# A three-block kernel on one Trainium2 core: the decay's sum as the exponential's bias, a scan scaled group by group, weight loads handed out later, and short products that fill TensorE's waits

## The chip, the cores and the metric

The kernel runs on one core of one Trainium2 chip. The metric is the device time of one execution in microseconds (us), the median over several runs. All tensors are float32.

## The reference, cut to what matters

The program computes two blocks. The first is attention plus a gated delta rule and a feed-forward layer over 256 tokens of width 1024. The second has two layers, each a mixer followed by a mixture of 16 experts; layer 0 works on 512 tokens (256 of context, 256 latent), layer 1 keeps the latent ones. Between the parts stand RMS norms. The change is for the most part in layer 0's mixer, a state-space scan in chunks of 128 tokens, run in both directions:

```python
la = (dt * a_neg).reshape(bsz, nc, SSD_CHUNK, ng, rep)
acum = jnp.cumsum(la, axis=2)
xdt = xs * dt[..., None]
to_end = jnp.exp(acum[:, :, -1:] - acum)
chunk_states = einsum("bcsgn,bcsgr,bcsgrp->bcgrpn", bc, to_end, xdt)
s_final, s_in = lax.scan(_carry_step, s0, (chunk_decay, chunk_states))
seg = acum[:, :, :, None] - acum[:, :, None, :]
decay = jnp.exp(jnp.where(causal, seg, -jnp.inf))
cb = jnp.einsum("bclgn,bcsgn->bclsg", cc, bc)
y_diag = jnp.einsum("bclsg,bclsgr,bcsgrp->bclgrp", cb, decay, xdt)
y_off = jnp.einsum("bclgn,bcgrpn,bclgr->bclgrp", cc, s_in, jnp.exp(acum))
return (y_diag + y_off), s_final
```

Beside it the kernel computes the modulation `silu(cond) @ mod_w + mod_b` of layer 1, whose weight is 24 MB.

## The kernel before, in words

**Stages.** The program is a chain of stages (`stage`, L227). A stage holds one instruction list per engine, with semaphores between them. Its end is a barrier for all engines (the branch at L231): the next stage starts when the slowest of TensorE, VectorE, ScalarE, GpSimd and SyncE has run its list, and SyncE's list is the issue of weight loads.

**Loads.** `Feed` has six slots of 1 MB. Every weight is cut into units of 1 MB, in the order in which TensorE takes them. `run` issues the units of one plan, each when the unit six before it has been used, and at its end `run_ahead` issues up to six units of the next plan (`most`). `run_part` (L310) does a piece of a plan that runs beside other stages. The modulation's plan is 24 units, two for each of 12 chunks of 512 columns (`modulate`, L2202). A chunk counts `mods_done` up by two when its products are done.

**The scan's four parts** (function `ssd`), in time order:
- Preparation: transposes, the step sizes `dt` (a softplus with chunks 0 and 1 of the modulation beside it), then a stage that makes the cumulated decay `acum` on TensorE with triangular matrices, copies it, and takes three exponentials. In that stage TensorE also does chunk 2, and SyncE issues modulation units 6 to 11.
- Main scan: 16 steps q = (t, g), four token tiles by four head groups. `prepare(q)` on TensorE makes C·B (L2320) and, for two directions and four heads, the decay's sum spread over rows (L2327). VectorE's `args(q)` subtracts the column's own sum and adds the causal mask, eight instructions of 128x128 (L2358). ScalarE takes two exponentials of 128x512 (L2387). VectorE multiplies by C·B (L2373), and TensorE makes 16 products of 64 columns (L2344) with `x_dt`, which VectorE makes for all 1024 columns of a tile when its first group comes up (L2368): it waits there until the last group's products have read the old one.
- State stage: eight steps n, each a chunk state, its decay and its part of the output; beside it modulation chunks 3 to 11 (`chunks_at`), three transposes of them (`turned_at`), and SyncE issues units 12 to 23 and six units of the output projection `ab_w_out`.
- `even_output`: gate, norm and output projection.

**Where TensorE waits.** `rmsnorm` (L467) has TensorE sum squares (L518), waits for root and reciprocal, and spreads the root (L523); with a residual VectorE then works for all eight tiles, without one and with `tail` the next stage does that part. `gated_head_norm` (L750) is the same per head. `route` chooses experts in a long VectorE chain and then counts in a stage of its own. At the end of `experts` the rows go to DRAM and come back gathered before TensorE turns them (L3115).

TensorE's granted clock has two levels here, 2.4 GHz (1.00 in the rows) and 1.2 GHz (0.50).

## Time and profile before

| what | value |
|---|---|
| median of 3 runs | 2445.96 us (2444.46 to 2446.03) |
| the profiled execution's own time | 2446.49 us |
| its span | 2444.7 us |
| TensorE busy, matmul | 2194.3 us (90%) |
| VectorE, ScalarE, GpSimd busy | 947.7, 483.3, 97.5 us |
| mean granted clock of TensorE | 0.946 of full speed |

How to read it: TensorE is busy nine tenths of the span, so an instruction saved on another engine is worth something only in a stage in which TensorE waits for that engine. A busy TensorE is not one at full speed: a clock of 0.50 in a stretch doubles each product. What a stage costs beyond that is read at its boundary, where the last engine's list ends.

### The profile page before, as it was taken

What the parts mean: (1) busy time and instruction counts of PE and PEld (TensorE: products, weight loads), DVE (VectorE), ACT (ScalarE), POOL (GpSimd) and SP (SyncE); (2) the same over time, 40 slices, a digit from 0 to 9 for tenths busy, and PEclk for the clock granted to TensorE, in tenths of its full rate; (3) what the DMA queues carried; (4) which work ended last, traced back from release to release, by engine and by line L of the source; (5) the groups of instructions that cost most, each with busy time, mean ns of one, the idle gap of its engine ahead of it and who ended that gap; (6) DMA issues with size and microseconds to landing.
All of it is one profiled execution on the core that took longest, in us unless ns stands there. A gap on an engine that the chain in (4) does not pass through costs nothing. (4 is left out here: it accounts for less than half of the span.)

```text
span 2444.7 us, 35746 instructions
## 1 busy us (share of the span) xinstructions
PE 2194.3 (90%) x14716; PEld 1546.8 (63%) x14716; DVE 947.7 (39%) x1997; ACT 483.3 (20%) x926; POOL 97.5 (4%) x122
## 2 busy tenths in 40 slices
PE   7999988798999889999787997999959999879884
PEld 6887887786888754444586444555537567745452
DVE  2267234312110239999485313211140555232112
ACT  0032522100000020003330102000031766121001
POOL 0000022100111000000000001000010000000000
PEclk8999999998999899999998998999969999989987
DMA  8443374243789622221308525999952222359993
GB/s 251 142 151 109 116 226 138 69 154 122 279 305 324 215 87 86 69 86 65 126 1 266 200 77 217 362 380 391 350 168 69 74 83 85 154 212 416 418 418 146
DMA packets 241237, 464.82 MB, mean 190 GB/s; under 512 B 14146, under 2 KB 195316, under 8 KB 216372
## 3 DMA queue, kind: packets, MB, share of 16 engines
q1 hardware_dynamic: 213120, 401.58, 46.6%
q0 software_dynamic: 12672, 46.14, 4.8%
q10 hardware_dynamic: 15284, 14.83, 1.9%
q8 instruction: 115, 1.88, 0.3%
q14 instruction: 46, 0.38, 0.0%
HBM read 412.84 MB, written 49.68 MB: 189 GB/s over the span
## 5 line engine op out<-in xcount | busy, mean ns | idle before, releaser
L2061 PE MATMUL bank<-hn,weights 128*128 128x512 f32 x640 | 277.5, 596 | 2.3 <-ACT hn L457 2.3
L2061 PEld LDWEIGHTS bank<-hn,weights 128*128 128x128 f32 x640 | 122.4, 191 | 156.0 <-issue 155.2
L2116 DVE SCALAR_TENSOR_TENSOR conv_sum<-mixer_then_weights_ahead,vec,conv_sum 128x572 f32<-128x572 f32 x240 | 175.0, 832 | 0.0
L625 PE MATMUL bank<-u,weights 128*128 128x256 f32 x768 | 170.8, 379 | 0.9 <-PEq L231 0.9
L3574 PE MATMUL bank<-hn,weights 128*128 128x512 f32 (+1 forms) x512 | 169.2, 488 | 0.0
L625 PEld LDWEIGHTS bank<-u,weights 128*128 128x128 f32 x768 | 144.8, 190 | 24.1 <-issue 5.4
L1655 PE MATMUL bank<-u,weights 128*128 128x256 f32 x704 | 155.6, 383 | 1.0 <-DVE u L438 1.0
L1655 PEld LDWEIGHTS bank<-u,weights 128*128 128x128 f32 x704 | 135.2, 192 | 19.9 <-issue 1.1
L3574 PEld LDWEIGHTS bank<-hn,weights 128*128 128x128 f32 x512 | 96.0, 190 | 65.3 <-issue 58.4
L2561 PE MATMUL bank<-mixer_then_weights_ahead,weights 128*128 128x512 f32 x256 | 110.6, 592 | 0.0
L3039 PE MATMUL bank<-weights,hn 128*32 128x128 f32 (+1 forms) x1344 | 99.8, 333 | 9.2 <-DMA weights<-in_moe_w_gate 6.7
L3240 DVE COPY hn<-bank 128x256 f32<-128x256 f32 (+1 forms) x41 | 15.4, 376 | 235.4 <-PE bank L3048 120.3
L3039 PE MATMUL bank<-mixer_then_weights_ahead,hn 128*64 128x256 f32 (+1 forms) x1120 | 99.0, 346 | 4.6 <-DMA mixer_then_weights_ahead<-in_moe_w_gate 4.6
L3039 PEld LDWEIGHTS bank<-weights,hn 128*32 128x32 f32 (+1 forms) x1344 | 62.6, 124 | 43.8 <-issue 22.3
L681 PE MATMUL bank<-u,weights 128*128 128x256 f32 x384 | 86.0, 388 | 4.7 <-DVE u L438 4.7
L3039 PE MATMUL bank<-weights_ahead,hn 128*32 128x128 f32 (+1 forms) x1120 | 74.2, 319 | 16.7 <-DMA weights_ahead<-in_moe_w_gate 13.9
L3039 PEld LDWEIGHTS bank<-mixer_then_weights_ahead,hn 128*64 128x64 f32 (+1 forms) x1120 | 62.3, 127 | 38.6 <-issue 12.0
L2561 PEld LDWEIGHTS bank<-mixer_then_weights_ahead,weights 128*128 128x128 f32 x256 | 48.3, 190 | 59.7 <-issue 59.7
L681 PEld LDWEIGHTS bank<-u,weights 128*128 128x128 f32 x384 | 74.9, 195 | 15.6 <-DVEq L689 4.9
L726 PE MATMUL bank<-ffn_hidden,weights 128*128 128x256 f32 x352 | 76.2, 379 | 1.9 <-PEq L231 1.9
L3039 PEld LDWEIGHTS bank<-weights_ahead,hn 128*32 128x32 f32 (+1 forms) x1120 | 47.5, 120 | 42.8 <-issue 24.1
L726 PEld LDWEIGHTS bank<-ffn_hidden,weights 128*128 128x128 f32 x352 | 66.8, 190 | 11.3 <-issue 2.3
(555 smaller groups left out, 3074.9 us busy)
## 6 DMA issues: line engine op xcount, KB each, us to landing
weights<-in_mod_w SPq DMA_DIRECT2D x48, 1024.0 KB, 8.0
weights<-in_w_in SPq DMA_DIRECT2D x36, 1024.0 KB, 5.3
token_rows<-o_b POOLq DMA_DIRECT2D x68, 512.0 KB, 7.6
weights<-in_moe_w_gate SPq DMA_DIRECT2D x24, 1024.0 KB, 25.1
weights<-in_moe_w_up SPq DMA_DIRECT2D x24, 1024.0 KB, 18.4
weights<-in_moe_w_down SPq DMA_DIRECT2D x24, 1024.0 KB, 20.0
weights<-in_ab_w_in SPq DMA_DIRECT2D x20, 1024.0 KB, 5.3
mixer_then_weights_ahead<-in_moe_w_gate SPq DMA_DIRECT2D x20, 1024.0 KB, 17.9
```

What stands on the lines that cost most here:

```text
L625: last = pe.matmul(bank(n), unit[:, k, m * P:(m + 1) * P], x(k), start=k == 0, stop=k == ktiles - 1)
L681: last = pe.matmul(kit.bank[n % 4][:, 0:T], unit[:, k, m * P:(m + 1) * P], x(k), start=k == 0, stop=k == DC - 1)
L726: last = pe.matmul(kit.bank[m][:, 0:T], unit[:, k, m * P:(m + 1) * P], x(at + k), start=at + k == 0, stop=at + k == total - 1)
L1655: last = pe.matmul(kit.bank[which + n % 2][:, 0:T], unit[:, k, m * P:(m + 1) * P], x(k), start=k == 0, stop=k == DC - 1)
L2061: last = pe.matmul(tile_bank(n)[:, :], unit[:, k, lane * P:(lane + 1) * P], hn[:, k, :], start=k == 0, stop=k == DC - 1)
L2116: ins = dve.scalar_tensor_tensor(s, x, w, s, ALU.mult, ALU.add)
L2561: last = pe.matmul(kit.bank[n % 4][:, 0:T2], unit[:, k, (n % 2) * P:(n % 2 + 1) * P], x(k), start=k == 0, stop=k == DC - 1)
L3039: last = pe.matmul(out, x[:, k, half, :], columns, start=half == 0 and k == 0, stop=half == 1 and k == 3)
L3240: dve.tensor_copy(ht[:, 0:4 * r], h_bank[:, 0:4 * r]).then_inc(h_copied, 1)
L3574: last = pe.matmul(bank, units[key][:, k, lane * P:(lane + 1) * P], hn[:, k, cols], start=k == 0, stop=k == DC - 1)
```

## The change

It has four parts.

1. **Decay.** The sum is kept negated (`minus_a_sum`). In the main scan VectorE only adds the mask, one 128x512 instruction per direction; the own sum enters as the bias of the exponential, so ScalarE has four of 128x128 per direction.
2. **x_dt by group.** Two instructions of 128x256 per step, made two steps ahead, in place of two of 128x1024 per tile.
3. **Loads and chunks.** Modulation units 6 to 13 are issued in the main scan's stage, 14 to 23 in the state stage, which issues only two units of `ab_w_out`; `feed.rest` issues the other four at the start of `even_output`. Chunk 3 is computed in the main scan at step 4.
4. **Fills.** `keep_busy` issues products of the identity with 256 columns, whose results nobody reads, at waits of TensorE.

```diff
+    def rest(self, sp):
+        _, per, source = self.plans[self.at]
+        for j in range(self.left, min(SLOTS, per)):
+            self.load(sp, source(0, j))
+        self.left = SLOTS
-    def run_part(self, sp, matmuls_done, first, last):
+    def run_part(self, sp, matmuls_done, first, last, most_ahead=SLOTS):
...
+def keep_busy(kit, pe, products, bank):
+    for _ in range(products):
+        pe.matmul(kit.bank[bank][:, 0:WIDE], kit.c("ident"), kit.const[:, 0:WIDE], start=True, stop=True)
@@ NormTail.wait (each norm with tail)
+        if c == 0:
+            keep_busy(self.kit, pe, 1, 5)
@@ rmsnorm, tensor
+                keep_busy(kit, pe, 1, 5)
                 for c in order:
...
                 last.then_inc(summed, 1)
+                keep_busy(kit, pe, 2, 5)
                 pe.wait_ge(inverted, 1)
...
                 last.then_inc(spread, 1)
+                if not tail:
+                    keep_busy(kit, pe, 6, 5)
@@ gated_head_norm, tensor: before the sums, and before the wait for the reciprocals
+                keep_busy(kit, pe, 2, 7)
...
+                keep_busy(kit, pe, 2, 7)
@@ ssd, the decay's sum
-                        v.link(dve, dve.tensor_copy(acum[:, :, :], ps))
+                        v.link(dve, dve.tensor_scalar(minus_a_sum[:, :, :], ps, -1.0, None, ALU.mult))
...
-                    @block.sync
-                    def _(sp):
-                        feed.run_part(sp, kit.mods_done, SLOTS, 2 * SLOTS)
@@ main scan
+                    @block.sync
+                    def _(sp):
+                        feed.run_part(sp, kit.mods_done, SLOTS, 2 * SLOTS + 2)
...
-                            pe.wait_ge(xdt_ready, t + 1)
+                            if q == 4:
+                                pe.wait_ge(y_copied, q)
+                                modulate(kit, pe, cond, 3, early_chunk(3))
+                            pe.wait_ge(xdt_ready, q + 1)
...
-                                for j in range(4):
-                                    at = d * 16 + 4 * g + j
-                                    ins = dve.scalar_tensor_tensor(m[:, q % 2, d, j, :], kit.bank[2 + 2 * (q % 2) + d][:, j * P:(j + 1) * P],
-                                                                   acum[:, t, at:at + 1], kit.c(("neg_f", "neg_r")[d]), ALU.subtract, ALU.add)
-                                ins.then_inc(args_ready, 1)
+                                dve.tensor_tensor(m[:, q % 2, d], kit.bank[2 + 2 * (q % 2) + d][:, :].rearrange("p (j n) -> p j n", j=4),
+                                                  kit.c(("neg_f", "neg_r")[d]).unsqueeze(1).broadcast_to([P, 4, P]), ALU.add).then_inc(args_ready, 1)
+                        def x_dt(q):
+                            t, g = steps[q]
+                            at = slice(g * 256, (g + 1) * 256)
+                            if q >= 4:
+                                dve.wait_ge(y_ready, q - 3)
+                            for d in range(2):
+                                ins = dve.tensor_tensor(by_head(xdt[:, d, at]), by_head(xt[:, t, at]),
+                                                        spread(dt[:, t, 16 * d + 4 * g:16 * d + 4 * g + 4], 4), ALU.mult)
+                            ins.then_inc(xdt_ready, 1)
...
-                                act.activation(m[:, q % 2, d], m[:, q % 2, d], ACT.Exp).then_inc(exp_ready, 1)
+                                for j in range(4):
+                                    at = d * 16 + 4 * g + j
+                                    ins = act.activation(m[:, q % 2, d, j, :], m[:, q % 2, d, j, :], ACT.Exp, bias=minus_a_sum[:, t, at:at + 1])
+                                ins.then_inc(exp_ready, 1)
@@ state stage
-                chunks_at = {0: (3,), 2: (4, 5), 3: (6, 7), 5: (8, 9, 10), 6: (11,)}
-                turned_at = {1: 0, 4: 1, 7: 2}
+                chunks_at = {1: (4, 5), 2: (6,), 3: (7,), 5: (8, 9), 6: (10, 11)}
+                turned_at = {0: 0, 4: 1, 7: 2}
...
-                        feed.run_part(sp, kit.mods_done, 2 * SLOTS, 2 * LATER_CHUNKS)
+                        feed.run_part(sp, kit.mods_done, 2 * SLOTS + 2, 2 * LATER_CHUNKS, 2)
@@ even_output, sync
+                feed.rest(sp)
                 sp.wait_ge(gated, DC)
@@ route: after the transposes; after the counts
+                keep_busy(kit, pe, 3, 6)
...
+                keep_busy(kit, pe, 2, 6)
@@ experts: at the start; at the end
+                keep_busy(kit, pe, 1, 0)
                 gather(0, 0, CAP)
...
                 pe.wait_ge(x_copied, count + (S + 1))
+                keep_busy(kit, pe, 24, 0)
                 pe.wait_ge(y_copied, count + S)
```

**What moves.** SyncE's list from the preparation's last stage to the output stage, before (a stage starts at the branch with a line of its own and ends at the branch L231; `L261` is a load into a slot of `Feed`):

```order
L2292 UNCONDITIONAL_BRANCH
L261 DMA weights<-in_mod_w 128x8x256 x6
L231 UNCONDITIONAL_BRANCH
L2411 UNCONDITIONAL_BRANCH
L261 DMA weights<-in_mod_w 128x8x256 x12
L261 DMA weights<-in_ab_w_out 128x8x256 x6
L231 UNCONDITIONAL_BRANCH
L2539 UNCONDITIONAL_BRANCH
L2857 DMA ven_mixer_then_weights_ahead<-in_moe_w_gate 128x2048 x2
L2857 DMA ven_mixer_then_weights_ahead<-in_moe_w_up 128x2048 x2
L2857 DMA ven_mixer_then_weights_ahead<-in_moe_w_down 128x2048 x2
```

and with the change:

```order
L2332 UNCONDITIONAL_BRANCH
L261 DMA weights<-in_mod_w 128x8x256 x8
L231 UNCONDITIONAL_BRANCH
L2445 UNCONDITIONAL_BRANCH
L261 DMA weights<-in_mod_w 128x8x256 x10
L261 DMA weights<-in_ab_w_out 128x8x256 x2
L231 UNCONDITIONAL_BRANCH
L2569 UNCONDITIONAL_BRANCH
L261 DMA weights<-in_ab_w_out 128x8x256 x4
L2890 DMA ven_mixer_then_weights_ahead<-in_moe_w_gate 128x2048 x2
L2890 DMA ven_mixer_then_weights_ahead<-in_moe_w_up 128x2048 x2
L2890 DMA ven_mixer_then_weights_ahead<-in_moe_w_down 128x2048 x2
```

The stage that held six modulation loads alone has no SyncE list any more; two loads moved from the state stage to the main scan, and four of `ab_w_out` to the stage after the next barrier.

VectorE in the main scan, before (`decay_cb<-bank,...` is the argument, `x_dt` the scaled x, `decay_cb<-decay_cb,c_b` the product with C·B):

```order
L2358 SCALAR_TENSOR_TENSOR decay_cb<-bank,a_sum,const 128x128 x8
L2368 TENSOR_TENSOR x_dt<-ven_mixer_then_weights_ahead,dt 128x1024 x2
L2373 TENSOR_TENSOR decay_cb<-decay_cb,c_b 128x512 x2
L2358 SCALAR_TENSOR_TENSOR decay_cb<-bank,a_sum,const 128x128 x8
L2373 TENSOR_TENSOR decay_cb<-decay_cb,c_b 128x512 x2
L2358 SCALAR_TENSOR_TENSOR decay_cb<-bank,a_sum,const 128x128 x8
L2373 TENSOR_TENSOR decay_cb<-decay_cb,c_b 128x512 x2
```

and with the change:

```order
L2381 TENSOR_TENSOR decay_cb<-bank,const 128x512 x2
L2390 TENSOR_TENSOR x_dt<-ven_mixer_then_weights_ahead,dt 128x256 x4
L2401 TENSOR_TENSOR decay_cb<-decay_cb,c_b 128x512 x2
L2381 TENSOR_TENSOR decay_cb<-bank,const 128x512 x2
L2390 TENSOR_TENSOR x_dt<-ven_mixer_then_weights_ahead,dt 128x256 x2
L2401 TENSOR_TENSOR decay_cb<-decay_cb,c_b 128x512 x2
L2381 TENSOR_TENSOR decay_cb<-bank,const 128x512 x2
```

Eight small instructions per step became two, and `x_dt` comes in pieces between the argument and the product.

TensorE at the end of the second `experts` and in the last norm, before (L3115 turns the gathered rows, L518 sums squares, L523 spreads the root, L393 turns the result):

```order
L3115 MATMUL bank<-const,weights_ahead 128x128 x16
L231 UNCONDITIONAL_BRANCH
L510 UNCONDITIONAL_BRANCH
L518 MATMUL bank<-squares,const 32x64 x32
L523 MATMUL bank<-rstd,const 128x64 x4
L231 UNCONDITIONAL_BRANCH
L385 UNCONDITIONAL_BRANCH
L393 MATMUL bank<-const,hn 128x128 x16
L231 UNCONDITIONAL_BRANCH
```

and with the change (L429 is a fill; L3150, L536, L542 and L400 are the four above):

```order
L429 MATMUL bank<-const 128x256 x24
L3143 REGISTER_ALU
L3150 MATMUL bank<-const,weights_ahead 128x128 x16
L231 UNCONDITIONAL_BRANCH
L527 UNCONDITIONAL_BRANCH
L429 MATMUL bank<-const 128x256
L536 MATMUL bank<-squares,const 32x64 x32
L429 MATMUL bank<-const 128x256 x2
L542 MATMUL bank<-rstd,const 128x64 x4
L429 MATMUL bank<-const 128x256 x6
L231 UNCONDITIONAL_BRANCH
L392 UNCONDITIONAL_BRANCH
```

A run of 24 fills stands before the turned rows, and one, two and six in the norm.

## Rows read from the trace of the kernel before

**Rows 1.** The page: its first line and TensorE's line of part 1.
```profile
span 2444.7 us, 35746 instructions
PE 2194.3 (90%) x14716; PEld 1546.8 (63%) x14716; DVE 947.7 (39%) x1997; ACT 483.3 (20%) x926; POOL 97.5 (4%) x122
```

**Rows 2.** By stretch: length, PE, PEld, DVE, ACT, POOL busy (count), clock, DMA share, GB/s.
```profile
1198.80:1207.50 8.70, 0.00 (x0) 0.00 (x0) 0.01 (x1) 0.00 (x0) 0.00 (x0) 0.71 1.09 348
1207.50:1282.70 75.20, 66.34 (x544) 65.32 (x544) 62.95 (x168) 27.93 (x64) 0.00 (x0) 0.93 0.10 30
1282.70:1340.30 57.60, 45.80 (x684) 38.07 (x684) 34.74 (x52) 1.98 (x5) 0.00 (x0) 0.87 0.80 256
```

**Rows 3.** Timeline at the first boundary: start us, duration us, engine, line; idle before.
```profile
1197.99 0.29 ACT L2300 ACTIVATE to_end<-to_end 128x128 f32<-128x128 f32 x1
1198.19 0.29 ACT L2301 ACTIVATE a_total_exp<-a_total_exp 128x128 f32<-128x128 f32 x1
...
1198.51 0.29 DVE L2280 TENSOR_TENSOR to_end<-to_end,dt 128x128 f32<-128x128 f32 x1 [0.78 <-ACT a_total_exp L2301]
...
1196.58 10.55 SPq L261 DMA_DIRECT2D weights<-in_mod_w  x3
```

**Rows 4.** Groups by line: count, busy us, mean ns of one, idle before.
```profile
L2358 DVE SCALAR_TENSOR_TENSOR decay_cb<-bank,a_sum,const 128x128 f32<-128x128 f32 x128 | 34.6, 344 | 11.9 <-PE bank L2327 11.9
...
L2387 ACT ACTIVATE decay_cb<-decay_cb 128x512 f32<-128x512 f32 x32 | 20.2, 632 | 40.3 <-DVE decay_cb L2358 40.3
...
L2373 DVE TENSOR_TENSOR decay_cb<-decay_cb,c_b 128x512 f32<-128x512 f32 x32 | 21.7, 687 | 1.2
...
L2368 DVE TENSOR_TENSOR x_dt<-mixer_then_weights_ahead,dt 128x1024 f32<-128x1024 f32 x8 | 9.4, 1221 | 3.2 <-PE bank L2344 3.2
...
L587 PE MATMUL bank<-hgrn_out,weights 128*128 128x256 f32 x128 | 27.9, 380 | 1.0 <-PEq L231 1.0
...
L1234 ACT ACTIVATE scores<-scores,softmax_small 128x128 f32<-128x128 f32 x8 | 3.2, 403 | 0.1
```

**Rows 5.** Timeline of the main scan on TensorE: products of groups, and its end.
```profile
1224.21 1.90 PE L2344 MATMUL bank<-x_dt,decay_cb 128*128 128x64 f32 x16
...
1228.01 1.90 PE L2344 MATMUL bank<-x_dt,decay_cb 128*128 128x64 f32 x16
...
1233.61 1.97 PE L2344 MATMUL bank<-x_dt,decay_cb 128*128 128x64 f32 x16 [1.64 <-issue]
...
1278.11 3.64 PE L2344 MATMUL bank<-x_dt,decay_cb 128*128 128x64 f32 x16 [1.49 <-issue]
```

**Rows 6.** Timeline of the state stage's last loads and the second boundary.
```profile
1327.20 18.11 SPq L261 DMA_DIRECT2D weights<-in_ab_w_out  x6
...
1324.32 2.74 PE L2208 MATMUL bank<-weights,cond 128*32 128x128 f32 x64 [3.09 <-DMA weights<-in_mod_w]
...
1345.76 3.62 PE L2552 MATMUL bank<-const,hn 128*128 128x128 f32 x16 [5.79 <-PEq L231]
```

**Rows 7.** By stretch, columns as in rows 2: stages that get fills.
```profile
470.40:484.70 14.30, 7.70 (x64) 6.46 (x65) 9.44 (x16) 4.67 (x10) 0.00 (x0) 0.76 0.01 1
571.10:594.90 23.80, 12.67 (x156) 10.28 (x157) 14.31 (x38) 4.04 (x11) 2.27 (x3) 0.57 0.27 94
...
1488.90:1502.80 13.90, 11.06 (x40) 7.29 (x42) 5.08 (x25) 0.00 (x0) 3.93 (x4) 0.51 0.23 93
...
1776.20:1792.10 15.90, 0.01 (x1) 0.03 (x1) 1.98 (x2) 1.24 (x1) 6.27 (x7) 0.60 0.90 282
...
2103.90:2116.40 12.50, 8.74 (x60) 7.50 (x53) 9.11 (x15) 1.79 (x6) 0.00 (x0) 0.60 0.00 1
...
2144.30:2175.20 30.90, 19.21 (x144) 11.15 (x146) 17.52 (x70) 9.15 (x19) 0.00 (x0) 0.67 0.42 174
2404.00:2416.40 12.40, 0.00 (x0) 0.00 (x0) 1.98 (x2) 1.24 (x1) 3.76 (x4) 0.63 0.56 181
2416.40:2444.70 28.30, 11.86 (x104) 9.85 (x104) 11.66 (x26) 5.08 (x9) 0.00 (x0) 0.56 0.11 42
```

More of the change, by code:

```diff
@@ L316, in run_part @@
         if last == per:
-            self.run_ahead(sp, per, lambda back: sp.wait_ge(matmuls_done, back + 1))
+            self.run_ahead(sp, per, lambda back: sp.wait_ge(matmuls_done, back + 1), most_ahead)
     def run_ahead(self, sp, units, used_up, most=SLOTS):
@@ L415, in _, with __init__ @@
                 act.copy(dst, src).then_inc(copied_a, 1)
+def keep_busy(kit, pe, products, bank):
+    for _ in range(products):
+        pe.matmul(kit.bank[bank][:, 0:WIDE], kit.c("ident"), kit.const[:, 0:WIDE], start=True, stop=True)
 class NormTail:
     SIGNALS = ("norm_scaled", "norm_by_a", "norm_by_v")
-    def __init__(self, x, root, parts, whole, by_vector):
+    def __init__(self, kit, x, root, parts, whole, by_vector):
+        self.kit = kit
         self.x, self.root, self.parts, self.whole = x, root, parts, whole
@@ L562, in rmsnorm @@
             if tail:
-                return NormTail(x, root, parts, whole, by_vector_last)
+                return NormTail(kit, x, root, parts, whole, by_vector_last)
 def project_programs(kit, x, ktiles, T, widths, evacuate):
@@ L1983 @@
 LATER_CHUNKS = 12
-MOD_EARLY = 3
 def even_units(ab):
@@ L2229, in ssd @@
             xt, bt = out.rearrange("p c t -> p (c t)").rearrange("p (t d) -> p t d", t=NT), new("b_tokens", NT, 512)
-            dt, la, acum, eac, etot, toend = [new(n, NT, 32) for n in ("dt", "log_decay", "a_sum", "a_exp", "a_total_exp", "to_end")]
+            dt, la, minus_a_sum, eac, etot, toend = [new(n, NT, 32) for n in ("dt", "log_decay", "minus_a_sum", "a_exp", "a_total_exp", "to_end")]
             turn(kit, [([xbc[:, c + j, t * P:(t + 1) * P] for j in range(4)], xt[:, t, c * P:(c + 4) * P])
@@ L2264, in ssd @@
                 softplus(kit, flat(dt[:, :, :]), flat(dt[:, :, :]), NT * 32,
-                         lambda pe: [modulate(kit, pe, cond, b, early_chunk(b)) for b in range(MOD_EARLY - 1)])
+                         lambda pe: [modulate(kit, pe, cond, b, early_chunk(b)) for b in range(2)])
                 with stage(nc, "la_ready", "sums_ready", "copied", "finished", "v") as (block, la_ready, sums_ready, copied, finished, vsem):
@@ L2289, in _ @@
                         last.then_inc(sums_ready, 1)
[L2290 to L2294 removed]
+                        modulate(kit, pe, cond, 2, early_chunk(2))
                     @block.scalar
@@ L2355, in args @@
                                     dve.wait_ge(y_ready, q - 1)
[L2356 to L2360 removed]
+                                dve.tensor_tensor(m[:, q % 2, d], kit.bank[2 + 2 * (q % 2) + d][:, :].rearrange("p (j n) -> p j n", j=4),
[9 more added lines that the diff above has]
+                            ins.then_inc(xdt_ready, 1)
                         args(0)
+                        for q in range(2):
+                            x_dt(q)
                         for q, (t, g) in enumerate(steps):
[L2364 to L2369 removed]
                             dve.wait_ge(cb_copied, q + 1)
@@ L2376, in _ @@
                                 args(q + 1)
+                            if q + 2 < len(steps):
+                                x_dt(q + 2)
                     @block.scalar
```

20 lines of the change are left out of this document (5 added, 15 removed).

## The prediction

> **What bounds the kernel now.** I read the page first: TensorE is busy 2194 of 2445 us [rows 1], so 250 us are left, and only an edit that shortens a wait of TensorE, removes its own work, or lifts its clock can show. Then I cut the span into stretches and looked for those where TensorE stands still or is granted half a clock. Three of them lie side by side in the scan. At the preparation's end TensorE does nothing for 8.70 us while DMA runs at 348 GB/s; the main scan takes 75.20 us at 30 GB/s, with TensorE busy 66.34 and VectorE 62.95; the state stage goes back to 256 GB/s with TensorE busy 45.80 of 57.60 [rows 2]. So loads bind the first and the third, and the one between has the DMA engines almost free. Last I read the timeline at the seams. At 1198.5 to 1198.8 the last real work of the preparation ends, but the issue of loads lasts from 1196.58 for 10.55 us, to 1207.1, and the barrier waits for it [rows 3]. At the second seam the six output loads are being issued for 18.11 us, to 1345.3, 3.0 us each, while TensorE's last product before is at 1327 and its next at 1345.76 [rows 6].
>
> **Part 1, the loads at the first seam.** The stage loses its SyncE list, so it ends with VectorE's last instruction at 1198.8 and not at 1207.1. Some 0.7 us of hand-over stay, as now (1207.1 to 1207.5, then the first product). That is **-8.0 us**. The eight loads that go into the main scan take 8 x 3.0 = 24 us of its 75, where nothing else is loaded; SyncE's list there ends after chunk 3, long before the stage does. What is late next at this seam is nothing: TensorE, ScalarE and VectorE end within 0.5 us of one another.
>
> **Part 2, the main scan.** Now TensorE sets the step: two groups of products stand 3.80 us apart (1224.21, 1228.01). Once per tile it waits for `x_dt`: the next group comes at 1233.61, 5.60 us later [rows 5], since both 1221-ns instructions [rows 4] start only when the old `x_dt` is read. Three tiles have this, 3 x 1.8 = **-5.4 us** once `x_dt` is made in pieces two steps ahead. The start of this stage runs at half clock after the idle 8.7 us (clock 0.71 there, 0.93 over the stage); without the idle most of this goes, **-2.5 us**. At the stage's end the last products take 3.64 us and not 1.90, at half clock [rows 5]; that should stay in part, and I take **-1 us**. Against this stands chunk 3, about 64 products, which takes 2.74 us at the clock of its row [rows 6] and some 2 at full clock, with half a microsecond of waiting: **+2.5 us**.
>
> Then the new pace. VectorE's step was eight of 344 ns (start to start about 0.27), two of 687 and a quarter of two 1221 [rows 4]: about 4.2 us in the mean. After it is two arguments at 0.69, two products at 0.69, and two pieces of 128x256 that I put at 0.42, between the two sizes: 3.6 us, under 3.80. ScalarE's chain is what may be late next. It had two of 632 ns. Now it has eight of 128x128 with a bias. One such takes 403 ns [rows 4]; two 128x128 of that engine without a bias start 0.20 us apart though each is 0.29 long, so 0.09 overlaps [rows 3], which gives 8 x 0.31 = 2.5 us, or with no overlap 3.2. The ends of the step's loop (argument of one direction 0.69, hops of about 0.3, product 0.64 to 0.69) run partly beside it. With overlap the loop is about 4.0 us against 3.80, which costs up to 3 us over 16 steps and may be hidden by the double buffer of `m`; without it, 4.9 us, or +13 in all. I take **+1**, nearest the row that shows overlap on the same engine, and keep -1 and +13 as ends. Part 2 is then -5.4 - 2.5 - 1 + 2.5 + 1 = **-5.5 us**.
>
> The Trainium skill ("VectorE: DVE Perf Modes", section "The TRN2 errata — SBUF-src ops pay a fixed extra latency per instruction") says that on trn2 each instruction of VectorE and ScalarE that reads SBUF pays a fixed cost, so that small tiles are dear; that speaks for the two wide arguments and against four exponentials in place of one. The 403 ns for a quarter of a 632-ns tile agree. The same notes ("ScalarE: Activation LUTs", section "Step-by-step: what each stage is for") put the overlap of two such instructions at about 93 ns, with which eight would take an estimated 2.45 us and the loop stays near TensorE's pace.
>
> **Part 3, the state stage and the second seam.** Now they last from 1282.7 to 1345.7, 63 us, and 18 loads of 3.0 us (54 us) with the wait for the first free slots fill them. After, ten modulation loads are due; they start when chunk 4 has freed slots, some 13 us in, and last 30 us. With the last load's landing (1.5), chunk 11 (2), its copy and the third transposing that makes about 48.5 us. The other chain there, VectorE's, had 34.74 us busy [rows 2] and waits for TensorE in each of eight steps, 45 us by estimate, just below. So **-14 us**, range -10 to -16. The four loads left go to the start of `even_output`, 12 us; the first two units are there, and one lasts TensorE 16 blocks by 512 tokens, 16 x 2 x 0.436 = 14 us (0.436 us for a product of 256 columns: 27.9 us / 64 pairs of records [rows 4]). I cost the loads at nothing; if that cover were gone, 3 to 6 us. After a shorter seam `even_output` starts warm: the 16 turns that took 3.62 us [rows 6] would take half, **-1.7 us**.
>
> Loads and scan together: -8.0 - 5.5 - 14 - 1.7 = **-29 us**, range -20 to -34.
>
> **Part 4, the fills.** A fill does no work; it can pay only by keeping TensorE's clock at 2.4 GHz for the products behind it. The most a stretch can give is its TensorE busy time less what it would be at full clock: busy x (1 - clock). From [rows 7] that is: a head norm 1.9, layer 0's residual norm 5.4, route 5.4, the next head norm 3.5, a long pair of norm and route 6.3 us, the last norm 5.2; 27.7 us, and some 7 more in two stretches of the first half that read like these. Not all comes. Head norms get two plus two fills for 6.6 us of standing still in several pieces: they should hold. In the residual norms the six fills last 6 x 0.436 = 2.6 us, less than half of VectorE's closing piece, which I estimate at 6 us of its 14.31 [rows 7], and the main scan lost its clock with idles of only 1.5 us [rows 5]; so some will still fall. The 24 fills last 10.5 us at full clock, against waits of 15.90 us in layer 0 and 12.40 us in layer 1 [rows 7]: in layer 0 5.4 us stay idle and the clock probably falls, in layer 1 2 us, and the norm behind it may start warm. I take half of the 34: **-17 us**. The low end: with the clock half anyway, a fill takes 0.87 us and stands ahead of work that is waited for. Six of them, 5.2 us, may outlast VectorE's closing piece where there is no residual, as at the last norm; 24 would take 20.9 us, 5 over the one wait and 8.5 over the other. At the norms that costs 0.4 to 2 us each.
>
> The sum is -29 - 17 = -46 us from the profiled execution's own 2446.5 us, which is 0.5 above the median: **2400 us**.
>
> **The rivals.** (A) The forecast, 62%: 2400, own range 2386 to 2413. (B) The fills give nothing: TensorE's clock falls in their gaps anyway and what they delay eats what they hold; 2446 - 29 = 2417 us. For it speaks the fall at the main scan's end with such short idles; against it that the main scan, with an idle of 1.64 us once per tile [rows 5], holds 0.93 over its length. 16%. (C) The fills hold nearly all, and the scan's part is at its best: 2446 - 34 - 28 = 2384 us, 12%. (D) The scan's part is small, because ScalarE's eight exponentials run without overlap (+12) or because the loads in the main scan reach back into steps; with the fills' 17 that gives 2446 - 17 - 17 = 2412, with weak fills 2422; 7%. (E) Slower: the 24 fills run at half clock in both layers. They begin after the last expert's products, while scatter and gather wait; if the clock falls before they end, the turned rows stand behind 20.9 us of fills, +5 and +8.5 us, and the norms lose 5 to 7 more; about +20. It decides only if parts 1 to 3 give less than that, for which the loads would have to be late by 10 us in the state stage. 2446 + 20 - 18 = 2448 at best, and to be over 0.2% above, 2452. 3%. That the change does not do what it says for the loads is excluded by the order of SyncE's list; for the fills it is rival B.
>
> **The numbers.** Likeliest 2400. The range takes A whole, B and most of D above and half of C below: 2378 to 2421. A measurement of this kernel can tell 0.2%, 4.9 us, from no change. Faster than that: A, B, C, D and a little of E, 0.95; within it 0.02; slower 0.03.
>
> **What would show it.** In the changed profile: the idle stretch of 8.7 us before the main scan is gone and the modulation loads lie beside it; groups of products stand 3.8 to 4.0 us apart with no 5.6 among them (4.9 throughout would be D); ScalarE's exponentials start 0.30 us apart; the state stage with its seam lasts 47 to 51 us; the output stage does not wait for its third unit. For the fills: granted clock of 0.9 and above in the head norms, 0.7 to 0.9 in the residual norms, and the gathered rows of the second layer turned at once after the wait. I am wrong in the main if the clock in the norms stays at 0.6, or if a stretch with fills is longer than before.

## The result, and the profile after

The changed kernel takes 2409.01 us, the median of four runs (2405.23 to 2412.61), against 2445.99 before (2444.46 to 2447.47). The ratio is 0.9848, 95% interval 0.9836 to 0.9860: 37 us faster, where 46 were forecast. The profiled execution took 2411.49 us, 2.5 above its median. Executions of one kernel differ by up to 13 us, so medians and intervals carry what follows, and one trace tells where time went, not to the microsecond how much.

The page of the changed kernel, beside [rows 1]:

```profile
span 2409.7 us, 36244 instructions
...
PE 2237.2 (93%) x14956; PEld 1578.7 (66%) x14956; DVE 936.1 (39%) x1925; ACT 502.1 (21%) x1021; POOL 97.7 (4%) x122
...
L429 PE MATMUL bank<-const 128*128 128x256 f32 x240 | 71.3, 438 | 29.7 <-PEq L231 20.8
```

TensorE is 43 us busier in a span that is 35 us shorter: 71.3 us of its work are fills. The three stretches of the scan, beside [rows 2], are the hand-over at the first seam, the main scan, and the state stage with the second seam (length, PE, PEld, DVE, ACT, POOL busy, clock, DMA share, GB/s):

```profile
1198.50:1200.50 2.00, 1.62 (x33) 1.12 (x25) 0.00 (x0) 0.00 (x0) 0.00 (x0) 0.50 0.00 0
1200.50:1269.00 68.50, 65.45 (x608) 64.73 (x608) 52.12 (x96) 47.29 (x160) 0.00 (x0) 0.95 0.39 124
1269.00:1322.20 53.20, 43.05 (x621) 35.67 (x621) 34.77 (x52) 1.86 (x5) 0.00 (x0) 0.90 0.75 238
```

The 8.70 us in which TensorE stood still are gone; the main scan went from 75.20 to 68.50 us with one chunk more in it; the state stage and seam went from 63 to 53. Inside the main scan, by timeline (products of groups) and by group of lines:

```profile
1210.80 1.90 PE L2369 MATMUL bank<-x_dt,decay_cb 128*128 128x64 f32 x16
...
1214.59 1.90 PE L2369 MATMUL bank<-x_dt,decay_cb 128*128 128x64 f32 x16
...
1264.55 3.65 PE L2369 MATMUL bank<-x_dt,decay_cb 128*128 128x64 f32 x16 [1.84 <-issue]
```

```profile
L2420 ACT ACTIVATE decay_cb<-decay_cb,minus_a_sum 128x128 f32<-128x128 f32 x128 | 39.2, 388 | 9.8 <-DVE decay_cb L2381 9.8
...
L2390 DVE TENSOR_TENSOR x_dt<-mixer_then_weights_ahead,dt 128x256 f32<-128x256 f32 x32 | 12.0, 419 | 0.0
```

The pace is 3.79 us, where [rows 5] have 3.80; none of the three gaps of 5.60 is left. One gap of 5.77 us stands in the scan, at step 4, and that is chunk 3:

```profile
1218.39 1.90 PE L2369 MATMUL bank<-x_dt,decay_cb 128*128 128x64 f32 x16
...
1224.16 2.00 PE L2369 MATMUL bank<-x_dt,decay_cb 128*128 128x64 f32 x16
```

One exponential is 388 ns long, and eight take 2.45 us, start to start 0.30, which is what the overlap in [rows 3] said. The clock still falls at the tail: 3.65 us for the last products, as before.

**Where the 35 us of the two traces lie.** I lined up the instructions of VectorE that both programs have. The difference of their start times (after less before) grows through a stretch by what that stretch gained. The same was done later for two experiments (the changed kernel without fills, the kernel before with fills alone):

| stretch (time before, us) | changed | no fills | fills alone |
|---|---|---|---|
| start to 1190 | -1.8 | -2.5 | -5.1 |
| first seam, with the start of the scan, to 1209 | -7.9 | -11.7 | -2.0 |
| main scan to 1283 | -3.9 | -5.0 | +1.6 |
| state stage and second seam to 1346 | -10.7 | -9.7 | +0.3 |
| `even_output` to 1460 | -0.7 | +1.2 | 0.0 |
| norm and route, layer 0, to 1505 | -1.5 | +1.1 | -1.5 |
| experts, layer 0, to 1640 | -1.5 | +1.2 | +2.3 |
| experts, layer 0, to 1765 | +3.5 | +0.2 | +1.0 |
| combining and norm, to 1830 | -0.3 | +1.7 | +1.1 |
| head norm, layer 1, to 2118 | -2.6 | -1.4 | -2.6 |
| norm and route, layer 1, to 2177 | -3.0 | +0.4 | -3.0 |
| experts and combining, layer 1, to 2422 | -1.2 | -0.2 | -1.9 |
| last norm | -2.2 | 0.0 | -2.1 |
| sum | -33.7 | -24.7 | -11.8 |

The table is one execution of each kernel. Entries of 1 to 3 us come and go: up to 1190 us the kernel without fills has the instructions of the kernel before, and its entry is -2.5 all the same. The execution of the fills alone that was traced, 2434.25 us, is 5 us faster than that kernel's median, so its sum of -11.8 is too good by as much. In the changed kernel's trace chunk 2 ran at half clock (0.50 in the first row above; it took 3.64 us, a chunk at full clock 1.95), which cost some 2 us at the first seam.

**The state stage** is one of the two terms that came short, the other being the fills (timeline of SyncE and TensorE):

```profile
1283.07 24.72 SPq L261 DMA_DIRECT2D weights<-in_mod_w  x10
```
```profile
1316.92 3.23 PE L2230 MATMUL bank<-weights,cond 128*32 128x128 f32 x64 [4.08 <-DMA weights<-in_mod_w]
...
1322.19 1.94 PE L2583 MATMUL bank<-const,hn 128*128 128x128 f32 x16 [0.68 <-PEq L231]
```

The first of ten loads is issued 14 us into the stage, when chunk 4 has freed its slots; chunk 11 waits 4.08 us for the last of them and then runs mostly at half clock (3.23 us in place of 1.95). The next stage starts 0.68 us after the barrier and warm, 1.94 us for the turns in place of 3.62 [rows 6].

**The stretches with fills**, beside [rows 7] in the same order (their six here: first head norm, residual norm, route of layer 0, combining of layer 0, norm and route of layer 1, last norm):

```profile
472.70:486.50 13.80, 9.33 (x72) 7.28 (x73) 9.35 (x17) 4.66 (x10) 0.00 (x0) 0.88 0.00 1
572.90:592.80 19.90, 15.33 (x183) 11.72 (x184) 14.30 (x38) 4.04 (x11) 2.27 (x3) 0.91 0.23 69
1463.60:1476.10 12.50, 12.13 (x46) 8.29 (x48) 5.10 (x25) 0.00 (x0) 2.98 (x3) 0.59 0.16 64
1751.50:1768.70 17.20, 13.23 (x50) 11.14 (x49) 1.98 (x2) 2.42 (x2) 7.27 (x7) 0.80 0.91 288
...
2116.80:2144.70 27.90, 21.71 (x164) 13.15 (x166) 17.52 (x70) 9.13 (x19) 0.00 (x0) 0.88 0.47 194
...
2386.00:2409.70 23.70, 11.99 (x122) 9.39 (x122) 11.66 (x26) 4.83 (x9) 0.00 (x0) 0.86 0.12 46
```

The clock rose in every one (0.57 to 0.91, 0.67 to 0.88, 0.56 to 0.86, but in layer 0's choice only 0.51 to 0.59). The first head norm gives 0.5 us, the combining of layer 0 is 1.3 us longer, counted to the first turned rows, and the others give 1.4 to 4.6.

The traces of all runs give this more firmly. Take eight of the stages that get fills: five norms or head norms, the choice of layer 0, the long pair in layer 1, and layer 1's combining with the last norm. From a stage's first instruction to the next stage's, the eight together take 164.2 to 168.3 us in the four kernels without fills (164.2 in the one that differs from the change by its fills alone) and 146.8 to 152.3 in the ten with fills (149.0 in the changed kernel). So inside their own stages the fills give about 15 us. The experiments show that less than that reaches the end.

### The profile page after: what moved, and what is told of

It reads as the page before. It is cut to its first block and busy times, and to the rows that moved or that the text cites. A ratio compares the mean times of both kernels' runs of the same rounds, so it can differ in the third digit from the quotient of the medians.

```text
span 2409.7 us, 36244 instructions
## 1 busy us (share of the span) xinstructions
PE 2237.2 (93%) x14956; PEld 1578.7 (66%) x14956; DVE 936.1 (39%) x1925; ACT 502.1 (21%) x1021; POOL 97.7 (4%) x122
## 5 line engine op out<-in xcount | busy, mean ns | idle before, releaser
L429 PE MATMUL bank<-const 128*128 128x256 f32 x240 | 71.3, 438 | 29.7 <-PEq L231 20.8
L429 PEld LDWEIGHTS bank<-const 128*128 128x128 f32 x240 | 47.9, 214 | 44.7 <-issue 33.7
```

The lines of the kernel that those rows point to most:

```text
L429: pe.matmul(kit.bank[bank][:, 0:WIDE], kit.c("ident"), kit.const[:, 0:WIDE], start=True, stop=True)
```

## The experiments

Each was timed beside the kernel before on the same chip, and its ratio is to that kernel. Its distance from the change is a difference of two medians. The intervals reach 3 to 6 us to either side, so a distance under some 5 us is not shown by the times, and has only the traces behind it. Theory at the start: loads and scan give about 25 us and do so through the two seams and the three stalls; fills give about 10, since a half clock costs only where TensorE sets the pace. Rivals: the fills are worth their forecast 17 or nothing, and the parts lean on one another.

**No fills.** `keep_busy` issues nothing.

```diff
-    for _ in range(products):
+    for _ in range(0):
```

> The changed kernel without any fill (240 matmul records of them gone). Theory, from the two traces: the fills give 9 to 11 us, all after the scan, since a half clock costs only where TensorE itself sets the pace; so 2418 to 2420 us, and the scan with both seams as in the changed kernel. Rival 1, the prediction's term: fills give 17 us, 2426. Rival 2: the fall of the clock is not stopped by them and the gain after the scan has another source: 2409 to 2412.

Measured: 2420.68 us (ratio 0.9897, 0.9880 to 0.9914). The fills give 11.7 us, loads and scan 25.2. The trace's mean clock is 0.949 against 0.970 with fills. As time at the half level that is 2 x 0.051 x 2419 = 247 us against 2 x 0.030 x 2410 = 145: **102 us of half clock were taken away for 12 us of time**.

**Fills alone** on the kernel before (all calls of `keep_busy`, nothing else).

> The kernel before with the fills alone. Theory: the same 9 to 11 us as when they are taken away from the changed kernel, 2435 to 2437 us. Rival 1: 17 us, 2429. Rival 2: nothing, or up to 3 us slower, 2446 to 2449, if what they give depends on the other parts.

Measured: 2439.27 us (0.9970, 0.9958 to 0.9981), a gain of 6.7. That is 2 to 4 us less than expected, and well under 17. The 6.7 and the 11.7 overlap in their intervals, so these runs do not show that the fills are worth more in the changed kernel.

**Loads alone**: part 3 of the change on the kernel before.

> The kernel before with the loads and chunks handed out as in the change (chunk 3 in the main scan, four output loads in even_output), but with the old decay, x_dt per tile and no fills. Theory: the first seam gives 8, the state stage with its seam 10, the warm start of two stages 3, chunk 3 takes 2.5: 2446 - 18 = 2427 to 2429 us. Rival (the prediction): the state stage shrinks by 14, 2423. Rival 2: x_dt stalls hide behind the loads, so that more is gained here and less by the scan's own part: below 2422.

Measured: 2427.45 us (0.9931, 0.9917 to 0.9944), a gain of 18.5, as the theory said.

**Scan alone**: parts 1 and 2 on the kernel before.

> The kernel before with the decay's sum as the exponential's bias and x_dt by group, loads and chunks as before, no fills. Theory: three stalls of 1.8 us go, the step stays at TensorE's 3.80 us: 2446 - 5.5 = 2440 to 2441 us, main scan 69 to 70 us in place of 75.2. Rival: the shorter scan only makes the state stage wait longer for its loads, so that the gain is given back: 2445 or more, with the main scan shorter all the same. Rival 2: the chain of eight exponentials sets the step, 3.9 to 4.2 us: 2443 to 2447.

Measured: 2439.82 us (0.9976, 0.9966 to 0.9986), a gain of 6.1. Its state stage is no longer than before (-0.3 us in the lined-up traces), so nothing is given back. 18.5 and 6.1 make 24.6 against the 25.2 of both: these parts add up.

**x_dt per tile** again, in the changed kernel.

```diff
-                            pe.wait_ge(xdt_ready, q + 1)
+                            pe.wait_ge(xdt_ready, t + 1)
...
-                            if q + 2 < len(steps):
-                                x_dt(q + 2)
+                            if g == 0:
+                                if t:
+                                    dve.wait_ge(y_ready, q)
+                                for d in range(2):
+                                    ins = dve.tensor_tensor(by_head(xdt[:, d, :]), by_head(xt[:, t, :]), spread(dt[:, t, 16 * d:16 * d + 16], 16), ALU.mult)
+                                ins.then_inc(xdt_ready, 1)
```

> The changed kernel with x_dt made per tile again, two instructions of 128x1024, the decay and the rest as changed. Theory: the three stalls of 1.8 us come back, and they alone: groups of products 5.6 us apart once per tile, main scan 5 to 6 us longer, 2414 to 2415 us. Rival: with the two wide arguments VectorE is 1 us per step earlier, so the stall shrinks to under 1 us each and the decay's edit is what gave the 6 us: 2409 to 2411.

Measured: 2413.90 us (0.9863, 0.9838 to 0.9888), 4.9 above the change; the intervals overlap. Timeline of TensorE at the first two changes of tile:

```profile
1217.02 1.96 PE L2230 MATMUL bank<-weights,cond 128*32 128x128 f32 x64
1218.91 2.00 PE L2369 MATMUL bank<-x_dt,decay_cb 128*128 128x64 f32 x16
...
1232.41 1.95 PE L2349 MATMUL bank<-const,log_decay 128*128 128x128 f32 x16
1236.00 1.97 PE L2369 MATMUL bank<-x_dt,decay_cb 128*128 128x64 f32 x16 [1.64 <-issue]
```

The stall of 1.64 us is back at the second change of tile, and so it is at the third: groups stand 5.60 us apart at both. At the first, chunk 3 stands in the stall and hides it, with 5.78 us against 5.77 in the changed kernel. So two stalls of 1.8 us come back, 3.6 us in all, and some 1.8 of the chunk's two microseconds would be free in this form.

**The old decay** with everything else as changed.

```diff
-                                dve.tensor_tensor(m[:, q % 2, d], kit.bank[2 + 2 * (q % 2) + d][:, :].rearrange("p (j n) -> p j n", j=4),
-                                                  kit.c(("neg_f", "neg_r")[d]).unsqueeze(1).broadcast_to([P, 4, P]), ALU.add).then_inc(args_ready, 1)
+                                for j in range(4):
+                                    at = d * 16 + 4 * g + j
+                                    ins = dve.scalar_tensor_tensor(m[:, q % 2, d, j, :], kit.bank[2 + 2 * (q % 2) + d][:, j * P:(j + 1) * P],
+                                                                   acum[:, t, at:at + 1], kit.c(("neg_f", "neg_r")[d]), ALU.subtract, ALU.add)
+                                ins.then_inc(args_ready, 1)
...
-                                for j in range(4):
...
-                                    ins = act.activation(m[:, q % 2, d, j, :], m[:, q % 2, d, j, :], ACT.Exp, bias=minus_a_sum[:, t, at:at + 1])
-                                ins.then_inc(exp_ready, 1)
+                                act.activation(m[:, q % 2, d], m[:, q % 2, d], ACT.Exp).then_inc(exp_ready, 1)
```

> The changed kernel with the old decay (eight arguments of 128x128 on VectorE, two exponentials of 128x512 on ScalarE) but x_dt by group. Theory: VectorE's step is then 8 x 0.27 + 2 x 0.69 + 2 x 0.38 = 4.3 us against TensorE's 3.80, so VectorE binds every step: 16 x 0.5 = 8 us more, 2416 to 2418 us, groups of products 4.3 us apart. The decay's edit would then gain nothing by itself and be what makes the other one possible. Rival: VectorE's waits leave it no room to bind and the stalls stay away: 2409 to 2411.

Measured: 2406.60 us (0.9849, 0.9831 to 0.9867). My theory fell: the kernel is as fast as the change, so the edit that the title names first gives nothing that can be measured. The same 35 us of the main scan in both, first with the old decay, then as changed:

```profile
1215.00:1250.00 35.00, 35.00 (x360) 34.61 (x360) 34.83 (x107) 15.46 (x34) 0.00 (x0) 1.00 0.26 83
```
```profile
1215.00:1250.00 35.00, 35.00 (x361) 34.68 (x361) 29.17 (x55) 26.47 (x91) 0.00 (x0) 1.00 0.35 111
```

With the old decay VectorE is busy for 34.83 of 35 us, but TensorE is too: the two are level. Groups of products stand 3.90 to 3.94 us apart in the first steps and 3.80 after chunk 3. I had added lengths (4.3 us); the engine overlaps the ends of its instructions, eight of 340 ns in 2.15 us, and its step is 3.90 to 3.94. That TensorE keeps 3.80 after chunk 3 fits the lead of two microseconds that the chunk gives VectorE, of which eleven steps of 0.1 us use about one; the old decay with `x_dt` by group and without chunk 3 was not tried. The edit buys room on VectorE (29.17 of 35) that nothing here uses.

**All six output loads** in the state stage (`most_ahead` left at six, no `feed.rest`).

> The changed kernel with all six output loads issued in the state stage again. Theory: 16 loads of 2.5 to 3.0 us from 14 us into the stage hold SyncE's list until 5 to 9 us after TensorE's end: 2414 to 2418 us. Rival: with the later start of the weights in even_output taken away something is gained back, or the list ends early enough: 2409 to 2411.

Measured: 2412.66 us (0.9866, 0.9851 to 0.9881), 3.7 above the change; the intervals overlap. Its SyncE and TensorE at the seam:

```profile
1303.63 18.03 SPq L261 DMA_DIRECT2D weights<-in_ab_w_out  x6
```
```profile
1316.59 0.69 PE L2479 MATMUL bank<-const,mixer_then_weights_ahead 128*128 128x128 f32 x4 [0.71 <-ACT mixer_then_weights_ahead L2502]
1322.11 3.65 PE L2582 MATMUL bank<-const,hn 128*128 128x128 f32 x16 [4.83 <-PEq L231]
```

The list ends at 1321.66, 4.4 us after TensorE's last product, and the next stage starts at half clock (3.65 against 1.94). At the seam this is 4.2 us more idle and 1.7 us more for the turns, so deferring four loads is worth 3.7 us by the medians and 5.9 by these rows. With them deferred, TensorE ends the stage and the ten other loads set its end, by way of chunk 11.

**The first transposing early.** In the state stage the three copied chunks are turned before the first chunk state, chunks 4 and 5 come right behind it, and the rest one per step.

```diff
-                chunks_at = {1: (4, 5), 2: (6,), 3: (7,), 5: (8, 9), 6: (10, 11)}
-                turned_at = {0: 0, 4: 1, 7: 2}
+                chunks_at = {1: (6,), 2: (7,), 3: (8,), 4: (9,), 5: (10,), 6: (11,)}
+                turned_at = {3: 1, 7: 2}
...
+                        turn_mod(0)
                         chunk_state(0)
+                        pe.wait_ge(columns_made, 2)
+                        for b in (4, 5):
+                            modulate(kit, pe, cond, b, mod_bank[:, (b % 4) * P:(b % 4 + 1) * P])
...
                         x_to_end(0)
+                        columns(0)
```

> The changed kernel with the state stage's first transposing of the modulation ahead of the first chunk state and chunks 4 and 5 right behind it, the later chunks one per step, and the second transposing in step 3. Theory: the ten loads of this stage bind it and start only when chunk 4 is done, 14 us after the stage's start; started at 6 to 7 us they end 7 us earlier and VectorE's chain (45 us) takes over: the stage with its seam 45 to 47 us in place of 53, 2402 to 2404 us. Rival: something else sets its end (the chain of VectorE is longer than I take it, or the loads run slower beside the steps): 51 to 54 us, 2408 to 2410.

Measured: **2398.73 us** (0.9803, 0.9782 to 0.9823), 10.3 below the change and 3 to 5 us better than expected. Its state stage, its loads and the wait of chunk 11:

```profile
1264.20:1308.60 44.40, 40.04 (x620) 33.59 (x621) 34.84 (x52) 1.83 (x5) 0.00 (x0) 0.96 0.89 284
```
```profile
1270.69 24.78 SPq L261 DMA_DIRECT2D weights<-in_mod_w  x10
```
```profile
1304.61 1.96 PE L2230 MATMUL bank<-weights,cond 128*32 128x128 f32 x64 [1.65 <-DMA weights<-in_mod_w]
```

The loads start 6.5 us into the stage in place of 14, chunk 11 comes 33.9 us after the first issue in both, and the stage takes 44.4 us in place of 53.2. So it was the moment at which chunk 4 frees its slots that set the stage, by way of the loads; that the later chunks also go one per step was not tried apart. Of the 12.8 us between the two traces 8.8 lie in this stage and 3.3 at the first seam, where chunk 2 was not slowed in this execution.

**Which fills count.** First the two runs of 24 are taken out, then all fills but those of the norms.

```diff
-                keep_busy(kit, pe, 24, 0)
```

> The changed kernel without the two runs of 24 fills; all others stay. Theory: in both layers the rows behind these fills are turned at the pace of the gathers and of VectorE's weighting, so their clock is worth nothing there; at most the norm behind loses 1 to 2 us in each layer: 2409 to 2412 us. Rival 1 (the prediction): layer 1's are worth 3 us and more, 2412 to 2415. Rival 2: they stand in the way of the turned rows, 2404 to 2407.

Measured: 2409.07 us (0.9846, 0.9821 to 0.9870), the change's own time within some 6 us.

> The changed kernel with the fills of the norms alone: none in the choice of experts, none at the start and end of the experts. Theory: what the fills gained in layer 0's choice of experts is given back where its weights' loads bind, the runs of 24 are worth 0 to 2, and only layer 1's choice of experts loses: 2410 to 2413 us. Rival: the fills there are worth what they showed in their own stretches (1.5 us in layer 0, 2 in layer 1, 1 to 2 at the ends): 2414 to 2416.

Measured: 2408.05 us (0.9845, 0.9823 to 0.9867). The fills in the choice of experts and in the experts give nothing that can be measured either, and this is 2 us below the range expected. The rows behind the 24 say why. Timeline of layer 0, before and with the change:

```profile
1792.11 1.94 PE L3115 MATMUL bank<-const,mixer_then_weights_ahead 128*128 128x128 f32 x8 [15.89 <-DVE mixer_then_weights_ahead L3299]
1795.38 1.97 PE L3115 MATMUL bank<-const,mixer_then_weights_ahead 128*128 128x128 f32 x8 [1.34 <-DVE mixer_then_weights_ahead L3299]
1797.95 1.97 PE L3115 MATMUL bank<-const,mixer_then_weights_ahead 128*128 128x128 f32 x8 [0.59 <-DVE mixer_then_weights_ahead L3299]
1800.71 1.97 PE L3115 MATMUL bank<-const,mixer_then_weights_ahead 128*128 128x128 f32 x8 [0.79 <-DVE mixer_then_weights_ahead L3299]
```
```profile
1755.51 13.39 PE L429 MATMUL bank<-const 128*128 128x256 f32 x48 [3.97 <-DMA hn<-token_rows]
...
1766.37 1.28 DVE L3334 SCALAR_TENSOR_TENSOR mixer_then_weights_ahead<-mixer_then_weights_ahead,weight_pair 128x1024 f32<-128x1024 f32 x1 [14.00 <-DMA mixer_then_weights_ahead<-token_rows,row_of_token]
...
1768.74 1.04 PE L3150 MATMUL bank<-const,mixer_then_weights_ahead 128*128 128x128 f32 x8
1770.47 1.10 PE L3150 MATMUL bank<-const,mixer_then_weights_ahead 128*128 128x128 f32 x8 [0.69 <-DVE mixer_then_weights_ahead L3334]
1773.03 1.09 PE L3150 MATMUL bank<-const,mixer_then_weights_ahead 128*128 128x128 f32 x8 [1.46 <-DVE mixer_then_weights_ahead L3334]
1775.80 1.97 PE L3150 MATMUL bank<-const,mixer_then_weights_ahead 128*128 128x128 f32 x8 [1.68 <-DVE mixer_then_weights_ahead L3334]
```

Eight products take 1.1 us in place of 1.97, but the third and the fourth eight start 2.56 and 2.77 us after the ones ahead of them, as they did before (2.57 and 2.76): VectorE hands the tiles over at that pace. A faster TensorE waits longer, and the fourth eight are at half clock again (1.97). The fills here also stand in the way a little. They begin 4 us late, behind a transfer, and end about 1 us after VectorE's first tile is ready, at 1767.65; VectorE's pace hides that too. In layer 0 the experts behind the choice are held by their weights. Waits of TensorE from 1690 to 1765 us of each trace, with the change and without fills (total, times, longest):

```profile
PE bank L3072 <- DMA mixer_then_weights_ahead<-in_moe_w_gate: 3.2, 1, 3.2
```
```profile
PE bank L3072 <- DMA mixer_then_weights_ahead<-in_moe_w_gate: 1.7, 2, 1.3
```

The table shows 3.0 us gained in choice and experts by 1640, and 3.5 given back by 1765. Part of that is this: TensorE comes earlier and waits longer for weights, 3.2 us at one stretch against 1.3 at most, and the longer wait is followed by half clock. It is not the fills' doing alone: the kernel with the scan's part and no fills gains 1.9 us by 1640 and gives back 3.7 by 1765, with one wait of 3.7 us for the same weights. How the rest divides was not tried.

**Two combinations.** The early transposing with norm fills alone, and the same with 13 fills in place of six in the two norms that add a residual.

```diff
-                    keep_busy(kit, pe, 6, 5)
+                    keep_busy(kit, pe, 6 if parts[0][4] is None else 13, 5)
```

> The early first transposing together with fills in the norms alone. Theory: the two are independent: 2398 to 2400 us, no slower than with all fills. Rival: with the experts' and the choice's fills gone layer 1 loses 2 to 4 us: 2401 to 2403.

> As the kernel with the early transposing and norm fills alone, but 13 fills in place of six in the two norms that add a residual, where VectorE works about 6.5 us after the spread root and TensorE stood idle for 3.7 us of it. Theory: the clock then stays at its full level into the next stage, 1 to 2 us less for each of the two norms: 2 to 3 us below the kernel with six. Rival: at this cover the clock falls at other places by its own run of luck, or the fills delay the next stage: within 1 us of it or slower.

Measured: 2403.54 us (0.9826, 0.9813 to 0.9840) with six, **2396.98 us** (0.9808, 0.9795 to 0.9822) with 13. Timeline of TensorE after the first residual norm's closing piece, with six and with 13:

```profile
577.79 2.81 PE L429 MATMUL bank<-const 128*128 128x256 f32 x12
584.34 1.19 PE L429 MATMUL bank<-const 128*128 128x256 f32 x2 [3.74 <-PEq L231]
```
```profile
575.98 5.83 PE L429 MATMUL bank<-const 128*128 128x256 f32 x26
582.52 0.67 PE L429 MATMUL bank<-const 128*128 128x256 f32 x2 [0.72 <-PEq L231]
```

Six leave 3.74 us idle, and the first fill of the next norm takes 1.19 us, at half clock; 13 leave 0.72 and it takes 0.67. In the lined-up traces the two norms gain 1.3 and 1.5 us by it. The medians differ by 6.6, more than the 2 to 3 expected and more than these two places explain, and the intervals overlap. The two traces are 10.2 us apart; beside the norms, 4.1 us lie in layer 0's experts up to 1765 and 2.3 in layer 1's norm and choice, where the two kernels have the same code. The first of the two missed its expectation: 2403.54 is 3.5 us above the theory and just past the rival's 2401 to 2403. Of the 2 to 4 us that the rival sees in layer 1, the trace shows 2.1 in norm and choice. Why it is slower, while norm fills alone cost nothing without the early transposing, is not settled: its interval overlaps that of the kernel with all fills (0.9813 to 0.9840 and 0.9782 to 0.9823). The best kernel is not clear of the one with the early transposing alone; both are some 10 to 12 us faster than the change.

## Why the prediction was right, and where it was off

The side, the likeliest case (A) and the range of 2378 to 2421 held; the sum of 46 us was 9 too large, 4 of them in the state stage and 5 in the fills. Of its own signs several did not come: the state stage with its seam lasts 53.2 us and not 47 to 51, the head norms stand at 0.88 and 0.85 and not at 0.9, and "a stretch with fills is longer than before", which was to show that it was wrong in the main, holds for the combining of layer 0 (15.90 to 17.20 us up to the first turned rows). By VectorE's instructions nothing is lost there, since VectorE sets the pace. By its terms:

- **First seam, -8.0, and the warm start, -2.5.** Right. Lined up, seam and start give 11.7 us where chunk 2 is not slowed, 7.9 in the trace where it is.
- **Main scan.** The three stalls: right, all are gone; undone, two of them come back (3.6 us in the trace, 4.9 by the medians) and chunk 3 hides the third. Chunk 3 took 2.0 us of the 2.5 charged. The pace: right at 3.80, with eight exponentials in 2.45 us against 2.5 worked out from the overlap in [rows 3]; the case without overlap (D) is excluded. One lasts 388 ns and eight 2.45 us, so (2.45 - 0.388) / 7 = 0.295 from start to start and 93 ns of overlap; by the figure of the Trainium skill ("ScalarE: Activation LUTs", section "What ACT_TABLE_LOAD costs", which is where the page has it and not in the section that the prediction names), about 93 ns, the trace agrees. The Trainium skill's rule that small tiles pay a fixed cost each ("VectorE: DVE Perf Modes", section "The TRN2 errata — SBUF-src ops pay a fixed extra latency per instruction") agrees with this trace too, 2.45 us for what two of 632 ns did. Part of those 2.45 us is the bias: one of this size lasts 388 ns with it and 0.29 us without [rows 3]. It costs no time, because ScalarE had 40.3 us of idle in this stage to pay it from [rows 4]. The term of -1 at the scan's tail was not there: 3.65 us, half clock, as before. Nor was the +1 for the pace. That these two errors cancel, so that the -5.5 stands beside the 6.1 of the scan's part alone, is luck.
- **State stage, -14 and -1.7.** The mechanism was right, the term mis-sized by 4: -9.8, and 53.2 us in place of 48.5. I took 31.5 us for ten loads and the landing of the last; from the first issue to chunk 11 it is 33.8, which the kernel with the early transposing repeats with 33.9. Chunk 11 at half clock is 1.2 more, and the first load comes after 14 us where I had 13. I also misread the seam before. TensorE's last product there does not end at 1327: that is one chunk of several [rows 6], and the last ends at 1339.98, 5.79 us before the turns, as their own row says. The sum does not use this. The greater miss is that I read the place of chunk 4 as given: moving it is worth 8.8 us in the stage and 10.3 by the medians, more than the whole of the scan's own part (6.1).
- **The fills, -17.** They give 11.7 us, and 6.7 on the kernel before. The bound was "the most a stretch can give is its TensorE busy time less what it would be at full clock", and half of it the guess. Inside the stages that guess was near, with 15.2 us in one pair of traces (164.2 less 149.0). The step that failed is the one behind it, that what a stage gains the whole kernel gains. The rows show three places where it does not: the turned rows, handed over at VectorE's pace; layer 0's experts, which wait for weights behind a choice that had gained 1.4 of its 5.4 us; and two places without fills that are slower in kernels with fills, told in the last section. In the residual norms some of the clock would still fall, the prediction said from the idle left, and that was right (3.74 us left).
- **Nothing for deferring four loads in `even_output`** was right: no wait for them shows at its start.
- **Rivals.** B (fills give nothing) and C (nearly all) lie on either side of 11.7 and both are out. E did not come: the 24 fills ran 13.39 us in layer 0, outlasting the wait by about 1 us, and 10.63 in layer 1, ending 2.18 us before it does, and taking them out changes nothing that can be measured.

## What to carry to other kernels

Find the first thing that a stage's loads wait for, not only how many loads there are: two chunks moved 7 us earlier were worth nearly as much as all 120 fills, and more than the decay and the split of `x_dt` together. Count half clock as a cost only for products whose successor does not wait for another engine or a transfer, and measure a fill by the whole kernel's time and not by its own stage. Where a fill is worth having, try how many the wait takes: here six left 3.74 us idle and the next norm began at half clock, 13 left 0.72 us and it did not. Before moving work off an engine, check with its real start-to-start pace that it is the one that binds.

## What was not expected of the hardware

In all ten kernels with fills TensorE's idle at the barrier inside the first block's feed-forward layer (755 us before) is 2.78 to 2.91 us; in the four without them (the kernel before among them) it is 1.62 to 1.91. In the changed kernel:

```profile
754.60 7.78 PE L747 MATMUL bank<-ffn_hidden,weights 128*128 128x256 f32 x28 [2.81 <-PEq L231]
```

Those 28 records take 7.78 us where they took 6.28 before, so the clock fell in the longer gap. Lined up, this place loses 2.4 to 2.7 us in nine of the ten, and 1.0 in the one with 13 fills, which loses 1.7 more just ahead of it. No fill stands near this barrier, and the work ahead of it is the same. It takes back most of the 3.1 to 4.1 us that six fills gain in the residual norm before it.

The stretch from 300 to 440 us, which has no fill either, is 1.3 to 4.6 us longer than before in nine of the ten kernels with fills, and in none of the three others. Nothing was tried on either place; their cause stays open.
